# The last output-projection chunk and the first feed-forward chunk computed by blocks of rows; the first feed-forward product's high and low parts regrouped

## What is computed

```python
    mix = jax.nn.sigmoid(ga) * (ya @ w_branch_a[l]) + jax.nn.sigmoid(gb) * (yb @ w_branch_b[l])
    h = h + rmsnorm(mix @ w_out[l], norm_attn_post[l])
    u = rmsnorm(h, norm_ff_pre[l])
    f = jnp.square(jax.nn.relu(u @ w_ff1[l])) @ w_ff2[l]
    h = h + rmsnorm(f, norm_ff_post[l])
```

## Time and profile before

| | us |
|---|---|
| median of 3 runs | 1389.99 (1388.82 to 1391.66) |
| the profiled execution, whole | 1388.86 |
| its span, first to last instruction | 1387.0 |
| TensorE busy | 1362.6 (98%) |
| VectorE busy | 759.8 (55%) |
| ScalarE busy | 627.8 (45%) |
| 16 DMA engines busy, mean | 60%, 182 GB/s |
| TensorE's granted clock over the span | 0.994 of full |

### The profile page before, as it was taken

How to read it: one execution, slowest core, us unless ns; L and a number is a source line. 1 busy time by engine, 2 the same in 40 slices (tenths; PEclk the granted TensorE clock), 3 DMA queues, 4 the chain that set the end, 5 groups by cost and what they waited for, 6 DMA issues and landing times.

```text
span 1387.0 us, 18451 instructions
## 1 busy us (share of the span) xinstructions
PE 1362.6 (98%) x6811; PEld 1111.1 (80%) x6811; DVE 759.8 (55%) x991; ACT 627.8 (45%) x915; POOL 51.4 (4%) x89
## 2 busy tenths in 40 slices
PE   7999999999999999998999999999999999999997
PEld 5876766777788888887888888888888888888886
DVE  5554544555565555554765554655545654556654
ACT  6544353454474444444544434444334443344442
POOL 1221120000000000000100000000000000000000
PEclk9999999999999999999899999999999999999999
DMA  8765464555556665776465656655666655666563
GB/s 223 223 177 150 134 167 136 156 150 159 142 167 189 191 190 187 233 253 211 135 200 184 196 169 213 188 190 188 192 186 189 188 191 191 196 184 188 191 196 108
DMA packets 130470, 253.08 MB, mean 182 GB/s; under 512 B 8547, under 2 KB 11039, under 8 KB 129932
## 3 DMA queue, kind: packets, MB, share of 16 engines
q1 hardware_dynamic: 126448, 241.28, 56.7%
q0 software_dynamic: 2192, 4.75, 1.7%
q10 hardware_dynamic: 1740, 5.88, 1.4%
HBM read 249.69 MB, written 2.17 MB: 182 GB/s over the span
## 4 chain that ended last, share of the span: by engine, by line
PE 98%; DVE 1%; DMA 0%; issue 0%; ACT 0%; POOL 0%; DVEq 0%; ACTq 0%; POOLq 0%
PE bank L1130 22%; PE bank L1131 21%; PE bank L1132 21%; PE bank L1407 17%; PE bank L1409 9%; PE bank L1148 1%; PE bank L1118 1%; PE bank L1243 1%; PE bank L1242 1%; PE bank L1287 0%; PE bank L1286 0%; DMA xm<-in_meta_tokens 0%; PE bank L1276 0%; PE bank L1274 0%; PE bank L1258 0%
## 5 line engine op out<-in xcount | busy, mean ns | idle before, releaser
L715 DVE TENSOR_TENSOR w_lo<-raw,w_hi 128x1024 fp32r<-128x1024 f32 (+1 forms) x456 | 550.7, 1214 | 455.8 <-ACT w_hi L378 454.2
L378 ACT ACTIVATE w_hi<-raw 128x1024 fp32r<-128x1024 f32 (+1 forms) x456 | 474.2, 1050 | 505.7 <-DMA raw<-in_w_ff 377.1
L1407 PE MATMUL bank<-f_hl,w_hi 128*128 128x512 f32 x1024 | 363.5, 400 | 1.5 <-issue 1.5
L1409 PE MATMUL bank<-f_hl,w_lo 128*128 128x256 f32 x1024 | 286.0, 282 | 0.0
L1407 PEld LDWEIGHTS bank<-f_hl,w_hi 128*128 128x128 f32 x1024 | 192.7, 189 | 48.1 <-issue 1.7
L1130 PE MATMUL bank<-w_hi,u_hi 128*128 128x512 f32 (+1 forms) x544 | 216.5, 398 | 1.4 <-DVE w_lo L715 1.4
L1131 PE MATMUL bank<-w_lo,u_hi 128*128 128x512 f32 (+1 forms) x544 | 209.4, 385 | 0.0
L1132 PE MATMUL bank<-w_hi,u_lo 128*128 128x512 f32 (+1 forms) x544 | 209.4, 385 | 0.0
L1132 PE MATMUL bank<-w_hi,hid_lo 128*128 128x512 f32 x512 | 199.2, 389 | 0.0
L1131 PE MATMUL bank<-w_lo,hid_hi 128*128 128x512 f32 x512 | 199.2, 389 | 0.0
L1130 PE MATMUL bank<-w_hi,hid_hi 128*128 128x512 f32 x512 | 199.2, 389 | 0.0
(11 more groups left out here) (194 smaller groups left out, 946.7 us busy)
## 6 DMA issues: line engine op xcount, KB each, us to landing
raw<-in_w_ff SPq DMA_DIRECT2D x256, 512.0 KB, 3.7
raw<-in_w_in SPq DMA_DIRECT2D x128, 512.0 KB, 3.6
raw<-in_w_out SPq DMA_DIRECT2D x32, 512.0 KB, 4.4
raw<-in_w_branch_b SPq DMA_DIRECT2D x16, 512.0 KB, 3.7
raw<-in_w_branch_a SPq DMA_DIRECT2D x16, 512.0 KB, 3.7
xs<-in_x SPq DMA_DIRECT2D x4, 512.0 KB, 10.9
raw<-in_w_in SPq DMA_DIRECT2D x8, 256.0 KB, 12.2
bias<-bias_table POOLq DMA_DIRECT2D x8, 256.0 KB, 4.5
```

Source lines behind the costliest of these rows:

```text
L378: act.activation(w_hi[:, u, :, 0:width], raw[:, u, :, 0:width], ACT.Copy).then_inc(hi_ready, 1)
L715: dve.tensor_tensor(w_lo[:, u, :, 0:width], raw[:, u, :, 0:width], w_hi[:, u, :, 0:width].bitcast(F32), ALU.subtract).then_inc(lo_ready, 1)
L1407: both = lambda: pe.matmul(acc[g][:], w_hi[:, u, k, cols], f_hl[:, kt, :], start=kt == 0, stop=kt == KT - 1)
L1409: low = lambda: pe.matmul(acc[g][:, 0:SEQ], w_lo[:, u, k, cols], f_hl[:, kt, 0:SEQ], start=False, stop=False)
```

## The change

**Output projection, last chunk.** It is computed in two passes over its eight units, first all products of row block 0 (48), then all of block 1, into banks 6 and 7. A new semaphore `out_rows` tells of the end of pass one; `used` is counted in pass two only. The chain of the first norm is done for each row block by itself (`square_last`, `root_out`, `keep_last`).

**The new stream** is made in eight pieces of one row block x 512 columns (`new_stream(n)`, n = 4 b + j), each turned by four transposes into bank 4 or 5. Pieces 0 to 3 are turned in pass two of the last output chunk, behind its units 2 to 5; pieces 4 to 7 in the first feed-forward chunk, at the places of `FIRST_TURNS`.

**Feed-forward, first chunk** (`first_chunk`). Pass one multiplies `w_hi` with the high and low columns of row block 0 (2 x 128 columns); pass two does the same for block 1 and multiplies `w_lo` with the 256 high columns. All are 256 columns wide: 64, then 128 products. Pass one waits for the high split of the weights alone. ScalarE's and VectorE's work at this place is written out in a fixed order; the squares of the new stream move to the second chunk, and the second norm's root to the third.

**First feed-forward product, other chunks** (`multiply_hidden`). For each step the four 512-wide products come in a row, then the four 256-wide ones (in the last step the other way round).

The diff, cut to its core:

```diff
+FIRST_TURNS = {(0, 4): 4, (0, 7): 5, (1, 1): 6, (1, 3): 7}
...
+        def piece(n):
+
+            return (rows, gate_b)[n // 2 % 2][:, n % 2, :]
...
+            def square_last(b):
+
+                if b:
+                    act.wait_ge(used, 8 * C_FF)
+                else:
+                    act.wait_ge(out_rows, 1)
+                act.activation(og[:, b, 3 * CW:], bank[6 + b][:], ACT.Square,
+                               accum_out=ss1[:, b * 4 + 3:b * 4 + 4]).then_inc(o_squared, 1)
+
+            def root_out(b):
+                act.wait_ge(norm, 4 + b)
...
-                    split_ahead(C_OUT + j, u)
-            square_out(3)
...
+                    if j < 3 or u < UNITS - LEAD:
+                        split_ahead(C_OUT + j, u)
...
+            def first_chunk():
+
+                square_last(0)
+                root_out(0)
+                keep_stream(0)
+                split_first(0)
+                keep_stream(1)
+                split_first(1)
+                keep_stream(2)
+                split_first(2)
+                keep_stream(3)
+                split_first(3)
+                square_last(1)
+                root_out(1)
+                split_first(4, 5, 6)
+                keep_stream(4)
+                split_first(7)
+                keep_stream(5)
+                keep_stream(6)
+                keep_stream(7)
+                for u in range(LEAD):
+                    split_hi(u, C_FF + 1)
...
+            def keep_last(b):
+
+                dve.wait_ge(o_squared, 6 + b + 1)
+                dve.tensor_reduce(ss1t[:, b:b + 1], ss1[:, 4 * b:4 * b + 4], AX.X, ALU.add).then_inc(norm, 1)
+                dve.tensor_tensor(og[:, b, 3 * CW:], bank[6 + b][:], g_post[:, 3 * CW:], ALU.mult)\
+                   .then_inc(acc_free, 1)
+                dve.wait_ge(acc_free, 2 * (C_FF - 1) + b + 1)
+                dve.wait_ge(stats, 13 + b)
+                link(dve.reciprocal(rstd1[:, b:b + 1], rstd1[:, b:b + 1]))
...
+            def first_chunk():
+
+                keep_last(0)
+                for n in range(4):
+                    new_stream(n)
+                keep_stream(0)
+                keep_stream(1)
+                keep_stream(2)
+                keep_stream(3)
+                split_first(0, 1)
+                keep_last(1)
+                new_stream(4)
+                new_stream(5)
+                keep_stream(4)
+                new_stream(6)
+                split_first(2)
+                keep_stream(5)
...
+            def turn_stream(n):
+                pe.wait_ge(hg_ready, n + 1)
+                if n >= 2:
+                    pe.wait_ge(turned_lo, T_H + n - 1)
+                turn4(bank[4 + n % 2], [piece(n)[:, k * P:(k + 1) * P] for k in range(4)]).then_inc(turned, 1)
...
+            pe.wait_ge(acc_free, 2 * (C_OUT + 2))
+            for b in range(BLOCKS):
+                for u in range(UNITS):
+                    ins = multiply(8 * (C_OUT + 3), u, *m, [bank[6], bank[7]], blocks=(b,))
+                    if b == 1:
+                        ins.then_inc(used, 1)
+                        if 2 <= u < 6:
+                            turn_stream(u - 2)
+                if b == 0:
+                    ins.then_inc(out_rows, 1)
...
-                    for g in range(4):
-                        cols = slice(g * P, (g + 1) * P)
-                        both = lambda: pe.matmul(acc[g][:], w_hi[:, u, k, cols], f_hl[:, kt, :],
-                                                 start=kt == 0, stop=kt == KT - 1)
-                        low = lambda: pe.matmul(acc[g][:, 0:SEQ], w_lo[:, u, k, cols], f_hl[:, kt, 0:SEQ],
+                    for wide in ((False, True) if kt == KT - 1 else (True, False)):
+                        for g in range(4):
+                            cols = slice(g * P, (g + 1) * P)
+                            if wide:
+                                ins = pe.matmul(acc[g][:], w_hi[:, u, k, cols], f_hl[:, kt, :],
+                                                start=kt == 0, stop=kt == KT - 1)
+                            else:
+                                ins = pe.matmul(acc[g][:, 0:SEQ], w_lo[:, u, k, cols], f_hl[:, kt, 0:SEQ],
                                                 start=False, stop=False)
...
+            def first_chunk():
+
+                pe.wait_ge(acc_free, 2 * (C_FF - 1))
+                halves = [f_hl[:].rearrange("p k (s t) -> p k s t", s=2)[:, :, :, b * P:(b + 1) * P]
+                          for b in range(BLOCKS)]
+                for b in range(BLOCKS):
+                    for u in range(UNITS):
+                        if b:
+                            pe.wait_ge(lo_ready, 8 * C_FF + u + 1)
+                        else:
+                            pe.wait_ge(hi_ready, 8 * C_FF + u + 1)
+                        pe.wait_ge(turned_lo, T_H + 4 * b + u // 2 + 1)
+                        for k in range(UK):
+                            kt = u * UK + k
+                            for g in range(4):
+                                cols = slice(g * P, (g + 1) * P)
+                                out = bank[g][:].rearrange("p (s t) -> p s t", s=2)[:, :, b * P:(b + 1) * P]
+                                ins = pe.matmul(out, w_hi[:, u, k, cols], halves[b][:, kt],
+                                                start=b == 0 and kt == 0, stop=False)
+                                if b:
+                                    ins = pe.matmul(bank[g][:, 0:SEQ], w_lo[:, u, k, cols], f_hl[:, kt, 0:SEQ],
+                                                    start=False, stop=kt == KT - 1)
+                        if b == 1:
+                            ins.then_inc(used, 1)
+                        if (b, u) in FIRST_TURNS:
+                            turn_stream(FIRST_TURNS[b, u])
```

More of the change, by code:

```diff
@@ L652, in quarter @@
                 for j in range(8):
+                    if first and j == 0:
+                        first_chunk()
+                        continue
                     for u in range(UNITS):
[L654 to L660, removed]
+                        if first and j == 1:
+                            square_h2(u)
+                        if first and j == 2 and u == 2:
+                            act.wait_ge(norm, 6)
                             act.activation(rstd2, ss2t, ACT.Sqrt, scale=1.0 / D, bias=eps).then_inc(stats, 1)
@@ L1014, in keep_stream, with new_stream @@
[L1014 to L1018 removed]
+                    if j < 3 or u < UNITS - LEAD:
+                        split_ahead(8 * (C_OUT + j), u)
+            def new_stream(n):
+                b, j = divmod(n, 4)
+                cols = slice(j * CW, (j + 1) * CW)
+                dve.scalar_tensor_tensor(h2[:, b, cols], og[:, b, cols], rstd1[:, b:b + 1], h2[:, b, cols],
+                                         ALU.mult, ALU.add).then_inc(hg_part, 1)
+                if n >= 4:
+                    dve.wait_ge(turned, T_H + n - 3 - UNTURNED)
+                dve.wait_ge(hg_part, n + 1)
+                dve.tensor_tensor(piece(n), h2[:, b, cols], g_ffpre[:, cols], ALU.mult).then_inc(hg_ready, 1)
@@ new lines, in keep_stream, with split_first @@
+            def keep_stream(n):
+                b, j = divmod(n, 4)
+                tiles = slice(4 * j, 4 * j + 4)
+                keep_lo(T_H + n, f_hl[:, tiles, SEQ + b * P:SEQ + (b + 1) * P],
+                        bank[4 + n % 2][:].rearrange("p (k t) -> p k t", k=4),
+                        f_hl[:, tiles, b * P:(b + 1) * P])
+            def split_first(*units):
+                for u in units:
+                    split_lo(u, 8 * C_FF + u + 1)
+            def first_chunk():
[14 more added lines that the diff above has]
+                keep_stream(5)
+                split_first(3)
+                new_stream(7)
+                split_first(4)
+                keep_stream(6)
+                split_first(5)
+                keep_stream(7)
+                split_first(6, 7)
+                for u in range(LEAD):
+                    split_lo(u, 8 * (C_FF + 1) + u + 1)
@@ L1410, in multiply_hidden @@
                                                 start=False, stop=False)
-                        for product in ((low, both) if kt == KT - 1 else (both, low)):
-                            ins = product()
                 ins.then_inc(used, 1)
+            def first_chunk():
[23 more added lines that the diff above has]
+                            turn_stream(FIRST_TURNS[b, u])
@@ L1441, in quarter @@
                             pe.wait_ge(hid_lo_ready, 4 + q * 4)
-                        if first and j == 0:
-                            pe.wait_ge(turned_lo, T_H + u + 1)
                         if j < 4:
```

94 lines of the change are left out of this document (29 added, 65 removed).

## The result

| | before | changed |
|---|---|---|
| median, us | 1389.4 (4 runs) | 1378.46 (1377.34 to 1380.25, 4 runs) |
| ratio to before | | 0.9925, 95% interval 0.9913 to 0.9937 |
| span of the profiled execution | 1387.0 | 1375.9 |
| TensorE's granted clock over the span | 0.994 | 0.998 |

A forecast was written before the change was run, and what follows sets the result against it. TensorE, holding 98% of the chain that ended last, was taken to bound the kernel. Gains of 7.4 + 4.8 = 12.2 us against the median of 1389.99 gave 1377.8 us, range 1375.4 to 1384.5.

The forecast's parts named there:

- The wait's after-effect: Behind TensorE's 4.80 us wait at the hand-over to the feed-forward: 8.1 us at half clock, about 4.05 us lost.
- Part 1: Hand-over from output projection to feed-forward by blocks of rows: 7.4 us gained, bounds 4 and 8.2.
- The wait for piece 2: In pass two TensorE waits for VectorE's low part of piece 0, as the PSUM bank is reused: about 0.5 us.
- E: Start of the last product of pass one in the last output projection chunk, put at 643.9 us.
- unit 7's high part: ScalarE's weight split in the first feed-forward chunk, ready about when TensorE asks: 0.3 us of wait, bounds 0 and 1.5.
- Part 2: First feed-forward product, 15 chunks, four wide then four narrow products: 4.8 us gained over 240 steps, bounds 0 and 6.4.
- a change of width: Between wide and narrow products, taken to cost the additional 7 ns; four changes become one, about 20 ns a step.
- The sum: Whole kernel: 7.4 + 4.8 = 12.2 us gained, giving 1377.8 us against the median.
- The order gives nothing: In the first feed-forward product, distances belong to wide and narrow products themselves; only 7.4 us gained: 1382.6 us, chance 0.27.
- new wait of 2 to 4 us: At the hand-over VectorE's line holds up piece 2 or 4, clock stays: 9.2 us gained, 1380.8 us, chance 0.13.
- the wait that only moves: VectorE reaches piece 0 or 4 late, TensorE stands over 3 us, clock falls: about 1386 to 1389 us, chance 0.05.
- The late weights: First feed-forward chunk's loads land 2.7 us apart, TensorE stands 6 us, clock falls: 1393 to 1394 us, chance 0.05.

The follow-up runs named there:

- the wait filled: The kernel before with 20 additional 512-wide products, results unread, on TensorE between output projection and first transposes: 1384.58 us, ratio 0.9975.
- the order alone: The kernel before with only the first feed-forward product reordered, four wide then four narrow products, in all 16 chunks: 1386.13 us, ratio 0.9981.
- alternating banks: The changed kernel with input projection, output projection and second feed-forward product reordered so the two row blocks alternate product by product: 1381.64 us, one run.
- runs of two: The changed kernel, first feed-forward product in two wide, then two narrow products: 1375.13 us into the same bank, 1376.9 into different banks, one run each.
- runs of eight: The changed kernel, first feed-forward product in eight wide, then eight narrow products, both steps of a unit together: 1376.15 us, one run.
- the hand-over alone: The changed kernel with the first feed-forward product back in its old alternating order: 1379.76 us, ratio 0.9944.

## Why the prediction was right, point by point

**What bounds the kernel.** Right: TensorE, its one long wait, and the distances between its products. What else paid was 0.5 us at the start of the middle quarters' second turn.

**The wait's after-effect.** Right in kind, the size was too large. The forecast said that 8.1 us passed at half speed and about 4.05 of them were lost; with the wait filled, 2.7 us came back by the trace, and 3 with the rhythm set aside. The 8.1 us held 0.68 of standing still, the slow work takes less than twice the time, and part of it covered a wait that then showed. This size was not a term of the sum, since that was made from the work at full clock.

**Part 1's sum.** 49.0 us of work and 0.8 of waits were forecast, 49.04 measured in all. The terms: the products were sized right (40 narrow ones from 657.34 to 662.13, 119.8 ns each, against 119). The transposes were over-sized: taking the products (21.8 and 23.0 us) and the wait of 0.64 us (0.87 less the ordinary 0.23) from 49.04 leaves 3.6 us for eight groups, 0.46 each, not 0.55. That is the lower of the two bounds, half of a group of eight. The wait for piece 2 was right in place and cause and nearly in size (0.5 forecast, 0.47 shown as idle). The line on VectorE behind it, to compare with the forecast's E (643.9; here 643.7):

```profile
645.90 0.75 DVE L1056 SCALAR_TENSOR_TENSOR h<-og,sc,h 128x512 f32<-128x512 f32 x1
646.69 0.69 DVE L1061 TENSOR_TENSOR rows<-h,g_ffpre 128x512 f32<-128x512 f32 x1
...
650.86 0.69 DVE L1061 TENSOR_TENSOR gate_b<-h,g_ffpre 128x512 f32<-128x512 f32 x1
651.47 1.28 DVE L771 TENSOR_TENSOR f_hl<-bank,f_hl 128x512 fp32r<-128x512 f32 x2
```

The first addition at E+2.2, the first low part at E+7.8: as worked out. The 0.3 us for unit 7's high part did not come up; no wait shows there. So part 1 gave 8.17 in place of 7.4, the upper of its bounds. With 0.47 for a group, the most that this part could give was 8.8 us and not 8.2; the wait of 0.64 took the difference.

**Part 2.** The step of the reasoning that failed is "if the additional 7 ns belongs to a change of width, four changes to and fro become one", 20 ns a step. The traces have 10: 1412 to 1402. A change of width is not one price: behind a run of four or more narrow products, each of the next four or five wide ones comes 2 to 9 ns late. The row that told so stood in the forecast and was set aside as an exception, the 233 ns between two wide products where chunks meet. It was the price in a run of four. The lower bound worked out from it, 1.4 us, lies nearer to the 2.2 measured than the 4.8 that was taken. The bounds themselves don't follow from the prices beside them. Four products at 231.5, four at 119 and one change at 9 ns make 1411 ns, a gain of 0.5 us and not 1.4; and the whole extra is 1413 - 1383 = 30 ns, 7.2 us and not 6.4.

**The sum** of 12.2 against 10.9 is thus 0.8 too little in part 1 and 2.6 too much in part 2 (partly one against the other), and the rest of 0.5 lies at the start of the second turn of the middle quarters' loop and in the opening. That the forecast came within 0.7 us of the measured time is luck in part: the reasoning of part 1 held, the one of part 2 did not, and their errors went opposite ways.

**The rivals.** "The order gives nothing" fell by the order alone (0.9981, interval below 1). Its argument, that the first chunk shows 346 ns with the same order, was sound for all that: alternation has two rhythms. The new wait of 2 to 4 us and the wait that only moves did not come. The first of these held that such a wait is "short enough that the clock stays"; the run with alternating banks speaks against that, for there the clock fell behind a wait of 1.8 us. The late weights did not either: the eight loads landed between 649.6 and 662.6 us by the trace, 1.9 us apart on the mean, and the only wait of ScalarE's for a landing that lay near the path was 0.7 us (unit 6):

```profile
661.38 1.06 ACT L385 ACTIVATE w_hi<-raw 128x1024 fp32r<-128x1024 f32 x1 [0.71 <-DMA raw<-in_w_ff]
```

It was done at 662.4 and wanted at about 663.5 (five units from 657.34 to 662.13, a turn, one unit more). Unit 7 was the close one, as worked out: its high part was done at 664.3, and TensorE came to it at about 664.4. So a tenth of a microsecond kept a further wait away.

## What to carry to other kernels

A hand-over in which a row-wise sum must be complete before the next product can begin costs the bounding engine more than its wait: here 5.5 us of standing still and some 3 us of half clock behind it. Splitting the last product by rows, so that one half's chain runs under the other half's work, took out all but 0.6 us, at a price of 64 products more (192 at 119.7 ns against 64 pairs at 346 to 353: 0.4 to 0.8 us, an estimate). Work the queue of the helping engine out step by step, in program order: the wait that stayed was found on paper to about a tenth of a microsecond, and moving one instruction took it away.

## What was not expected of the hardware

- TensorE's distance from product to product depends on what ran before, beyond each product's own width. Wide (512) and narrow (256) products mixed cost 25 ns a step of eight above the plain sum in turns of one, 7 in runs of two, 15 in runs of four, 9 in runs of eight. The bank made no difference in runs of two (1394 ns both), nor the moving operand in runs of eight, where the last three wide products are 227 ns apart like those with weights as moving operand.
- The same alternating code runs at 346 ns a pair or at 353 and stays there over dozens of pairs. It was seen to change behind a turn (in the kernel before at 681 us, from 346 to 353) and where chunks meet. In the kernel with the hand-over alone two chunks behind the loop's jump are fast, from 1015 to 1060 us (five pairs from 1039.67 to 1041.41, 348 ns each):

```profile
1039.67 0.39 PE L1489 MATMUL bank<-f_hl,w_hi 128*128 128x512 f32 x1
...
1041.41 0.39 PE L1489 MATMUL bank<-f_hl,w_hi 128*128 128x512 f32 x1
```

- The opening differs from execution to execution: the last output chunk's first product stood between 632.2 and 634.4 us in the twelve traces. By its size this could be most of the scatter of the runs; that was not tested.
- A wait of 1.8 us of TensorE was followed by 3.4 us at a granted clock of 0.50 (banks alternate elsewhere, one trace); in the other traces, waits of 0.4 to 1.1 us behind 650 us that began at a clock of 1.00 were followed by 1.00.
